# A fused decoder-step kernel: feature chunks placed by shares of the time line, one-page products on GpSimd, and the block inversion's operands in PSUM

## What is computed

```
proj = rms(x) @ w_in                      # 4*512 attention, 4*512 DeltaNet, 8 gate, 2*1024 merge columns
attention, prompt:  4 heads, 1024x1024 causal, two softmaxes per head, p1 - lam * p2
attention, samples: 8 sequences x 32 pages of 128 cached tokens, keys and values from the page table
DeltaNet, prompt:   short convolution; 8 tiles of 128 tokens; per tile and head a lower
                    triangular system (I + L) is solved; then a scan over the tiles carries the state s
DeltaNet, samples:  one recurrent update per sequence
y = sigmoid(ga) * (o_a @ w_up_a) + sigmoid(gb) * (o_b @ w_up_b);  out = x + y @ w_out
```

## Time and profile before

| what | us |
|---|---|
| median of three runs | 1423.93 |
| the profiled execution's own time | 1425.43 |
| its span, first to last instruction | 1423.6 |
| TensorE busy in the span | 1290.7 (91%) |
| VectorE busy | 679.4 (48%) |
| GpSimd busy | 427.7 (30%) |
| ScalarE busy | 295.5 (21%) |

### The profile page before, as it was taken

One profiled execution on the slowest core, in us unless ns is written; L12 is line 12 of the kernel. 1 busy time (PEld: TensorE's weight loads), 2 busy tenths in 40 slices (PEclk: granted clock), 3 DMA queues, 4 the chain that ended last, 5 costly groups with the idle time before them and its releaser, 6 DMA issues.

```text
span 1423.6 us, 20555 instructions
## 1 busy us (share of the span) xinstructions
PE 1290.7 (91%) x7189; PEld 659.0 (46%) x7189; DVE 679.4 (48%) x938; ACT 295.5 (21%) x649; POOL 427.7 (30%) x232
## 2 busy tenths in 40 slices
PE   7999999989988989998989984699998969999999
PEld 3444344544454454454445442355555534554443
DVE  2756106647667758665556568235342104522101
ACT  3111013424334334232212100112111111110000
POOL 1123104525324434346557633435520000000000
PEclk9999999999999999999999997899999989989999
DMA  7221408664784774677997994876872554360221
GB/s 231 79 94 47 141 1 272 199 211 141 244 270 138 248 243 144 212 253 249 333 325 246 356 362 142 224 258 234 261 256 78 176 176 128 119 235 31 72 76 60
DMA packets 167179, 269.23 MB, mean 189 GB/s; under 512 B 29618, under 2 KB 66297, under 8 KB 165916
## 3 DMA queue, kind: packets, MB, share of 16 engines
q1 hardware_dynamic: 107636, 149.64, 33.2%
q10 hardware_dynamic: 59440, 118.28, 24.7%
HBM read 221.63 MB, written 46.40 MB: 188 GB/s over the span
## 4 chain that ended last, share of the span: by engine, by line
PE 33%; DVE 5%; issue 4%; DMA 3%; ACTq 3%; SPq 2%; ACT 1%; POOL 0%; DVEq 0%; POOLq 0%
PE ps L1669 11%; PE ps L1976 8%; PE ps L1953 5%; PE ps L1692 2%; DVE qkv L1408 2%; SPq L611 1%; PE ps L1781 1%; ACTq L892 1%; ACTq L895 1%; DMA work<-in_cache_v 1%; PE ps L1784 1%; DVE vbuf L1406 1%; DVE sc L1252 1%; PE ps L1926 1%; PE ps L1913 1%
## 5 line engine op out<-in xcount | busy, mean ns | idle before, releaser
L1669 PE MATMUL ps<-hT,wbuf 128*128 128x512 f32 x1152 | 556.9, 618 | 0.3 <-ACT fst L933 0.3
L1669 PEld LDWEIGHTS ps<-hT,wbuf 128*128 128x128 f32 x1152 | 211.5, 197 | 203.7 <-issue 198.9
L709 POOL TENSOR_TENSOR prod<-work,qB 128x1024 f32<-128x1024 f32 x64 | 157.6, 2467 | 189.5 <-DVE sc L1252 76.0
L709 POOL TENSOR_TENSOR prod<-kbuf,qB 128x1024 f32<-128x1024 f32 x64 | 153.0, 2394 | 131.8 <-DVE sc L1252 95.9
L1586 PE MATMUL ps<-wbuf,hT 128*128 128x512 f32 x384 | 169.4, 599 | 1.1 <-ACT qkv L798 1.1
L1252 DVE TENSOR_REDUCE sc<-prod 128x16 f32<-128x1024 f32 x128 | 154.7, 1211 | 15.0 <-POOL prod L709 14.1
L1586 PEld LDWEIGHTS ps<-wbuf,hT 128*128 128x128 f32 x384 | 72.5, 191 | 89.6 <-issue 88.0
L1976 PE MATMUL ps<-hT,work 128*128 128x512 f32 x256 | 110.3, 592 | 0.0
L1953 PE MATMUL ps<-qkv,wbuf 128*128 128x512 f32 x192 | 92.3, 636 | 14.8 <-issue 10.6
L1976 PEld LDWEIGHTS ps<-hT,work 128*128 128x128 f32 x256 | 48.5, 190 | 60.7 <-issue 60.7
L1692 PEld LDWEIGHTS ps<-work,pr 128*2 128x2 f32 x2048 | 46.2, 84 | 64.8 <-issue 55.2
(11 more groups left out here) (325 smaller groups left out, 1342.6 us busy)
## 6 DMA issues: line engine op xcount, KB each, us to landing
work<-in_cache_v ACTq DMA_DIRECT2D x256, 256.0 KB, 4.1
kbuf<-in_cache_k SPq DMA_DIRECT2D x128, 256.0 KB, 3.7
work<-in_cache_k SPq DMA_DIRECT2D x128, 256.0 KB, 4.0
wbuf<-in_w_main ACTq DMA_DIRECT2D x10, 2048.0 KB, 9.7
gsp<-work SPq DMA_DIRECT2D x24, 512.0 KB, 5.3
feat_dram<-qkv ACTq DMA_DIRECT2D x20, 512.0 KB, 4.5
qkv<-in_x_prompt SPq DMA_DIRECT2D x16, 512.0 KB, 4.9
feat_dram<-fst ACTq DMA_DIRECT2D x32, 256.0 KB, 3.1
```

The lines of the kernel that those rows point to most:

```text
L709: nc.gpsimd.tensor_tensor(prod[:, p % 4:p % 4 + 2, :], kpair[u], qB[:, j % 2:j % 2 + 1, :].to_broadcast([P, 2, W]), ALU.mult).then_inc(s[" ...
L1669: ins = nc.tensor.matmul(ps[:, 4 + n % 2, :], wbuf[:, wb, kk, f * P:(f + 1) * P], hT[:, kk, half_ * W:(half_ + 1) * W], start=(kk == 0), s ...
```

## The change

It has three edits.

- `slot(j, k)` now counts work: each slot is 67/16 units, and `filled` finds the time by which so much work is done when chunks get 0.72 of the line up to 440, 0.95 up to the first key tile, 0.45 through the key tiles, 0.95 from `INVERT` to the first `solve`, 0.52 through solve and scan, and 0.95 after it. All chunks but the first begin 8 units of work earlier. `INVERT` stays; VectorE's inversion moves from `INVERT` + 3 to + 12, `solve_at` from + 66 to + 75, with 22.5 between tiles in place of 23; what hangs on the inversion on SyncE moves from + 58 to + 66.5.
- GpSimd multiplies one page of 512 columns per instruction, and each adds 1 to `page_mul`; it waits for the reduction and the load once per pair, as before.
- `BN` is copied by VectorE into PSUM banks 2 and 3 (`BP`), and `outer` lies in bank 7. So in each of the 62 instructions of the inversion one of the two inputs is in PSUM.

```diff
--- before.py
+++ after.py
@@ -180,7 +180,6 @@
     bbaT = work[0:8, 0:TOK]
     qf = qkv[:].rearrange("p c t n -> p (c t n)")
 
-    kpair = [kbuf[:, 2 * u:2 * u + 2, :] for u in range(RING // 4)] + [work[:, 2 * u * W:2 * (u + 1) * W].rearrange("p (a n) -> p a n", a=2) for u in range(RING // 4)]
     kslot = [kbuf[:, u, :] for u in range(RING // 2)] + [work[:, u * W:(u + 1) * W] for u in range(RING // 2)]
     vslot = [work[:, 2048 + u * W:2048 + (u + 1) * W] for u in range(RING)]
     kf, vf, pf, wf = (t[:].rearrange("p a n -> p (a n)") for t in (kbuf, vbuf.rearrange("p a h n -> p a (h n)"), prod, wbuf.rearrange("p a k n -> p a (k n)")))
@@ -223,7 +222,8 @@
 
 
     BN, XB = (qf[:, i * 1024:(i + 1) * 1024].rearrange("p (j i) -> p j i", j=32) for i in range(2))
-    outer = vf[:, 0:256]
+    outer = ps[:, 7, 0:256]
+    BP = psf[:, 1024:2048].rearrange("p (j i) -> p j i", j=32)
     Xc, Yc = (qf[:, 2054 + i * 1024:3078 + i * 1024].rearrange("p (e n) -> p e n", n=32) for i in range(2))
     Yf = [qf[:, 4102 + u * 512:4614 + u * 512].rearrange("p (h n) -> p h n", h=AH) for u in range(2)]
     Xf = [qf[:, 5126 + u * 256:5382 + u * 256].rearrange("p (h n) -> p h n", h=AH) for u in range(2)]
@@ -325,12 +325,6 @@
 
     SLOTS = 16
     ROWS = 20
-    starts = [110 * j if j < 4 else 440 + 96 * (j - 4) for j in range(NF + 1)]
-
-    def slot(j, k):
-
-        return starts[j] + k * (starts[j + 1] - starts[j]) / SLOTS
-
     def row_at(i):
 
         return slot(i // AH, 4 * (i % AH) + 4)
@@ -345,10 +339,26 @@
     INVERT = keys_at(NT) + 4
 
     def solve_at(c):
-        return INVERT + 66 + 23 * c
+        return INVERT + 75 + 22.5 * c
 
     def scan_at(c):
         return solve_at(c) + 14
+
+    SHARE = ((440, 0.72), (keys_at(0), 0.95), (INVERT, 0.45), (solve_at(0), 0.95), (solve_at(NT), 0.52), (2000, 0.95))
+    STEP = 67 / SLOTS
+
+    def filled(work):
+
+        t = 0
+        for end, share in SHARE:
+            if work <= (end - t) * share:
+                return t + work / share
+            work -= (end - t) * share
+            t = end
+
+    def slot(j, k):
+
+        return filled((SLOTS * j + k) * STEP - (8 if j else k / 2))
 
     def stages(chunk, rows, attention, gates, invert, solve, scan):
 
@@ -571,7 +581,7 @@
             yield INVERT + 2
             for c in range(2):
                 scan_load(c)
-            yield INVERT + 58
+            yield INVERT + 66.5
             sp.wait_ge(once("x_inv"), nth("x_inv"))
             sp.dma_start(xd_dram.rearrange("e b i k -> (e b) (i k)"), XB.rearrange("p j i -> p (j i)")).then_inc(s["sp_st"], 16)
             sp.wait_ge(s["sp_st"], 16 * 1)
@@ -697,16 +707,17 @@
 
 
         def chunk(j):
-            for p in range(0, NPAGE, 2):
+            for p in range(NPAGE):
                 yield slot(j, p / 2) - 4.5
                 if scores(j):
-                    u = p % RING // 2
+                    u = p % RING
                     if p == 0:
                         po.wait_ge(s["qb_in"], 16 * (j + 1))
                     if j * NPAGE + p >= 4:
-                        po.wait_ge(s["page_red"], j * NPAGE + p - 2)
-                    po.wait_ge(s[f"kin{u}"], j * 128 + p // RING * 32 + 32)
-                    nc.gpsimd.tensor_tensor(prod[:, p % 4:p % 4 + 2, :], kpair[u], qB[:, j % 2:j % 2 + 1, :].to_broadcast([P, 2, W]), ALU.mult).then_inc(s["page_mul"], 2)
+                        po.wait_ge(s["page_red"], j * NPAGE + p // 2 * 2 - 2)
+                    if u % 2 == 0:
+                        po.wait_ge(s[f"kin{u // 2}"], j * 128 + p // RING * 32 + 32)
+                    nc.gpsimd.tensor_tensor(prod[:, p % 4, :], kslot[u], qB[:, j % 2, :], ALU.mult).then_inc(s["page_mul"], 1)
 
         def attention(h):
             yield head_at(h, 7) + 29.5
@@ -1390,26 +1401,27 @@
                                     h3(Dm).unsqueeze(2).to_broadcast([P, AH, 2, P]), ALU.mult).then_inc(s["lq_done"], 1)
 
         def invert():
-            yield INVERT + 3
+            yield INVERT + 12
             dve.wait_ge(s["mask_in"], 48)
             dve.wait_ge(s["kqg_st"], 16 * NT)
             dve.wait_ge(s["kgv_st"], 16 * NT)
             dve.wait_ge(s["lq_st"], 80 * NT)
             link(nc.vector.tensor_reduce(own, ident[:].rearrange("p (b n) -> p b n", b=4), AX_X, ALU.add))
             nc.vector.memset(Sst, 0.0).then_inc(s["s_done"], 1)
+            nc.vector.tensor_copy(BP, BN)
             link(nc.vector.memset(XB, 0.0))
             link(nc.vector.memset(XB.rearrange("p j i -> p (j i)")[:, 0:1024:33], 1.0))
             for j in range(31):
                 n, m = 31 - j, j + 1
-                yield INVERT + 4 + 1.7 * j
+                yield INVERT + 13 + 1.7 * j
                 o3 = outer[:, 0:n * m].rearrange("p (n m) -> p n m", n=n)
-                link(nc.vector.tensor_tensor(o3, BN[:, j, j + 1:32].unsqueeze(2).to_broadcast([P, n, m]),
+                link(nc.vector.tensor_tensor(o3, BP[:, j, j + 1:32].unsqueeze(2).to_broadcast([P, n, m]),
                                              XB[:, j, 0:m].unsqueeze(1).to_broadcast([P, n, m]), ALU.mult))
                 ins = nc.vector.tensor_tensor(XB[:, j + 1:32, 0:m], XB[:, j + 1:32, 0:m], o3, ALU.subtract)
                 if j < 30:
                     link(ins)
             ins.then_inc(once("x_inv"), 1)
-            yield INVERT + 62
+            yield INVERT + 70.5
             dve.wait_ge(s["xc_in"], 64)
             nc.vector.transpose(Yc.rearrange("p e n -> p (e n)"), Xc.rearrange("p e n -> p (e n)")).then_inc(once("yc_done"), 1)
 
```

## The result

The changed kernel takes 1428.5 us (median of 20 runs), the kernel before 1424.6 (20 runs beside them): ratio 1.0031, 95% interval 1.0018 to 1.0043. The forecast was 1391, range 1364 to 1426, with 0.77 on faster. It was wrong in sign, and the time lies just outside its range. Two of the 20 executions had a lower granted clock (1468.9 us at 0.906, 2205.4 us at 0.556) and are left out of the ratio; the median of the other 18 is 1427.9. The profiled execution took 1426.0 us, its span is 1424.1.

The account below looks back on a forecast made before the run. The prediction took TensorE as the bound, so that only its idle time could be gained. Attention +47, key tiles -33, inversion -6, solve and scan -25 and tail -16 gave -33 us: 1391 us, range 1364 to 1426.

Parts of the forecast that it names:

- GpSimd's pages, 0: GpSimd's one-page products: a pair takes 2.19 us against 2.355, and neither gain nor loss reaches TensorE; 0 us.
- Key tiles: Key tiles: features leave and a tile falls from 22 us to about 17.6; -33 us, ends 20 and 37.
- Attention, +47: Attention: 0.94 chunk more adds 59 us of TensorE work, of which idle takes a third, 12 us; +47 us.
- the slower rival: Attention is paced by the chunk, 100 us each, not by TensorE's work; sum +14, time 1438; chance 0.14.
- the much faster rival: Features fill all 36 us of TensorE's idle in attention, +23 in place of +47; time 1367; chance 0.12.
- Solve and scan, -25: Solve and scan: TensorE is busy 95%, so features that leave shorten it; -25 us, ends 15 and 30.
- the term that kept 5 us for a solve's dependent steps: Solve and scan: fewer features stand between a solve's dependent steps, so 5 of the 30 us are kept.
- Tail, -16: Tail after the scan: 17 records of features left in place of 47; -16 us, ends 10 and 17.
- Inversion, -6: Inversion: PSUM operands shorten VectorE's steps to 21.5 us, while more chunk enters; stage 86 to 80 us, ends 74 and 92.
- the rival by which steps still wait for GpSimd: Inversion: the PSUM edit fails, the chain stays at 57 us or more; +3 in place of -6, 1400; chance 0.06.
- The term that was set at nothing: Inversion: SyncE's wait for the finished inverse has later slots' key pages behind it, GpSimd can use four ring slots; 0 us.
- No change: the chains hold their rounds: Key tiles and scan: chains hold their rounds once features leave, giving only -13 and -12; time 1424; chance 0.09.

Follow-up runs that it names:

- e1_lead: The changed kernel with both pages of a pair at the pair's place in GpSimd's queue, 4.5 ahead; 1394.9 us, ratio 0.9795 to the kernel before.
- e2_pair: The changed kernel with GpSimd's product as before, one instruction for two pages; 1410.4 us, ratio 0.9886 to the kernel before.
- e5_slots_only: The kernel before with only the new line of chunks, two-page products and the inversion's operands in SBUF; 1419.6 us, ratio 0.9962.
- e3_psum_only: The kernel before with only the inversion's blocks and outer products in PSUM; 1413.0 us, ratio 0.9921.
- e8_lead_sbuf: The changed kernel with both pages at the pair's place and the inversion's operands back in SBUF; 1407.0 us, ratio 0.9858 to the kernel before.
- e9_key_share: The changed kernel with both pages at the pair's place and chunk shares 0.69 up to 440, 0.55 in key tiles; 1399.1 us, ratio 0.9832.

## Why the prediction was wrong

It forecast 47 - 33 - 6 - 25 - 16 = -33. By events the changed kernel has +48, +9, 0, -37 and -18, that is +2. The miss is mainly in one term, the key tiles, by 42 us, with 6 in the inversion; the scan gives 12 back.

**The step that failed: "GpSimd's pages, 0".** It priced the halved product by its duration and by GpSimd's busy share, and put the cover at "neither gain nor loss reaches TensorE". It did not ask where the second product of each pair now stands in GpSimd's queue, what it has ahead of it there (a chain step that itself waits for VectorE), and what stands behind the reduction that waits for it (the same chain, on VectorE). A moved step was costed as one that stays. What the runs show in its place is 40.3 us of reductions waiting for that second page in the key tiles; e1_lead, which only moves the page forward, takes the wait to 0.2 us and the stage from 179.4 to 148.9. The answer was in the text of the change: 4.5 against half of 67 / 16 / 0.45. Busy shares can't show it, as nobody is short of time here.

**Key tiles.** With the lead mended they fall by 21 us (170.1 to 148.9), against 33 forecast and a lower end of 20. The rounds of e1_lead, 16.8 to 21.8, include those of 17 to 18 that were asked for, and three of seven from 19 to 22, as at the lower end. The bound "wrong if key rounds stay above 20" was met by the changed kernel, with 20.7 to 27.8.

**Attention, +47: right** (+48; +46 to +48 in the two runs of the mended kernel). From the second on, sample projections stand 92 to 98 us apart while attention runs (105 to 107 before), against 90 to 95. So the slower rival, a chunk at 100 us, falls: 0.94 chunk cost 48 us and not 94. One credit in it was missed: the shorter product saves 13 us (e2_pair), so with two-page products the stage would have grown by 59 to 61, all that the added work costs with no idle filled. TensorE's idle in the stage says the same: 40 us before, 38 in e2_pair and e5_slots_only, 29 in after. The features filled next to nothing, the shorter waits did. So the sum came out right by luck, with two errors that cancel, and the much faster rival, by which features fill all 36 us, falls.

**Solve and scan, -25: under-sized.** -37 in after, -34 to -39 in those two runs; the bound was 30. The features that left are 63 records, about 0.49 chunk or 31 us at 63. TensorE's busy time fell by 35 us and its idle did not grow, it stayed at 11 to 12 us in both tables; the term that kept 5 us for a solve's dependent steps standing open had nothing to keep. First solves follow each other after 18 to 26 us (24 asked for). **Tail, -16**: -18.

**Inversion, -6: 0.** The PSUM edit did what the prediction said: 21.2 us for the steps (21.5 forecast), none over 0.43, the copy 1.21. The rule of the Trainium skill's page "VectorE: DVE Perf Modes", section "The TRN2 errata", by which they would take some 4.0 more (an estimate), is not seen: a step of 255 columns takes 420 ns undisturbed in SBUF (line 1406 before) and 422 from PSUM (line 1418 after), and the 62 steps have 21.2 us in e3_psum_only too. So the rival by which steps still wait for GpSimd falls. The wait for line 1264's instruction is gone, and the first solve waits 5.28 us in place of 12.79. But the chain from the blocks to the inverse falls only from 56.9 to 51.4 us (879.3 to 930.7): two reductions more in it, 2.4 us, and 8.8 us of reductions waiting for products in place of 0.8, the longest 7.80 us. That product had waited for its key page:

```profile
893.81 2.49 POOL L720 TENSOR_TENSOR prod<-kbuf,qB 128x512 f32<-128x512 f32 x2 [13.20 <-DMA kbuf<-in_cache_k]
```

And what follows the inverse grew from 16.0 to 24.6 us (to 955.3). SyncE's queue after shows that, in the columns of a timeline:

```profile
931.11 3.98 SPq L474 DMA_DIRECT2D work<-in_cache_k  x4
935.13 0.44 SPq L586 DMA_DIRECT2D xd_dram<-qkv  x1
944.41 3.85 SPq L590 DMA_DIRECT2D qkv<-xd_dram  x4
949.01 2.71 SPq L474 DMA_DIRECT2D kbuf<-in_cache_k  x3
```

and before:

```profile
886.16 0.33 SPq L576 DMA_DIRECT2D xd_dram<-qkv  x1
890.46 4.40 SPq L580 DMA_DIRECT2D qkv<-xd_dram  x4
```

The inverse is ready at 930.7, but four key pages of the next slots are issued first, until 935.1, and then its store lands 9.3 us after its issue, where it took 4.3 before. The DMA engines are full meanwhile (a recorded share of 1.06, and 0.93 before); in e5_slots_only and e8_lead_sbuf, where they are 0.50 busy at that moment, the store lands in 2.6 us. The term that was set at nothing ("SyncE's wait for the finished inverse ... I cost it at nothing") looked at what lies behind that wait, not at what lies ahead of it, nor at a full DMA: 8.6 us.

That the stage would be shorter without this detour is not shown: a kernel with the store placed ahead of the pages was not tried, and e9_key_share speaks against it. There the store goes out as soon as the inverse is ready, and the first solve follows after 12.9 us, but the chain takes 63.3 us and the stage 87.1. In all seven runs with the new line and PSUM the stage is 84 to 87 us, with chains from 51.1 to 63.3, and the DMA engines are 0.94 to 0.98 busy at 326 to 338 GB/s. The bytes are those of the prediction (28 to 29 MB), but it had them move at 388 GB/s. So DMA may be what sets this stage now; that was not tried either, and which of the two makes this term's miss stays open.

**The rivals.** "No change: the chains hold their rounds" comes nearest in its time and its place, but by a mechanism that the prediction did not have: the chains can run at 17 to 22 us a tile (e1_lead), and it was the order of one queue that kept them from it. With that order mended, the time is 1395 to 1399, where 1391 was forecast. That nearness is in part luck: the key tiles then miss by +12 us and the inversion by +6, solve and scan by -9 to -14.

## What to carry to other kernels

When an instruction is split in a kernel whose order is written by times, ask of each half where it now stands in its in-order queue, what that queue waits for ahead of it, and what is queued behind the instruction that consumes it; a lead given as a constant must be set against the slot's longest length, not its mean. Where a stage grows while every engine in it idles more, go to the groups' idle times and look for two engines that wait for each other in order. And price a VectorE step with two SBUF inputs on a chain by the longest GpSimd instruction that can run beside it (here up to 2.44 us, against 0.2 to 0.4 alone): put an operand into PSUM, or make the GpSimd instruction shorter.

## What was not expected of the hardware

A product of 128x512 takes 1.27 us here, not the 1.094 of line 733's: a pair takes 2.50 to 2.54 us where one of 128x1024 took 2.355. Columns: shortest, median and longest ns, first and last start; line 720 after.

```profile
L720 POOL TENSOR_TENSOR prod<-kbuf,qB x128: 1256/1268/2258, 152.7 to 1006.7; 128x512 f32<-128x512 f32 x128
```

Splitting GpSimd's work costs it 0.15 to 0.18 us a pair and still saved 13 us of attention, through the engines beside it (e1_lead against e2_pair). That is a gain which GpSimd's own rows cannot show.
